# Work moved from the first expert pair to behind the seventh, and constants moved in the load order, in a hybrid attention and mixture-of-experts step

## The reference

```python
scores = sigmoid(t @ w_router)            # 64 experts, 8 picked for each token
a = silu(t @ w_exp_gate[e]) * (t @ w_exp_up[e]) * gate[e]
routed = sum_e a @ w_exp_down[e]          # 1024 -> 256 -> 1024 for each expert
shared = (silu(t @ w_sh_gate) * (t @ w_sh_up)) @ w_sh_down
return routed + shared
```

## Time and profile before

| | us |
|---|---|
| median of 3 runs | 787.26 (786.84 to 790.26) |
| profiled execution | 786.93 |
| its span | 785.1 |
| TensorE busy | 742.6 (95%) |
| VectorE busy | 383.4 (49%) |
| ScalarE busy | 136.3 (17%) |
| DMA | 268.72 MB, mean 342 GB/s |

### The profile page before, as it was taken

The page is one execution under the profiler, slowest core; times in us unless marked ns, Lnnn a source line. Parts: engine busy times, 40 slices in busy tenths (PEclk is TensorE's granted clock), DMA queues, the critical chain, the costliest instruction groups (busy, mean ns, idle before and its releaser), DMA issues.

```text
span 785.1 us, 13758 instructions
## 1 busy us (share of the span) xinstructions
PE 742.6 (95%) x5059; PEld 357.3 (46%) x5059; DVE 383.4 (49%) x869; ACT 136.3 (17%) x290; POOL 42.9 (5%) x49
## 2 busy tenths in 40 slices
PE   4999999889999999999999999899999999999988
PEld 0554434566555454544444444344444443444433
DVE  2236368483786334454454354344543454435456
ACT  3124001410111121111111111111110111111110
POOL 0000001000000110110100101101001011010100
PEclk9999999999999999999999999999999999999999
DMA  9993465650818969999999999999999999999992
GB/s 342 386 386 141 172 237 233 243 175 21 312 33 349 355 241 383 399 420 419 418 419 421 418 422 418 418 421 418 421 419 419 421 417 421 419 419 421 419 389 84
DMA packets 52218, 268.72 MB, mean 342 GB/s; under 512 B 6556, under 2 KB 8988, under 8 KB 27104
## 3 DMA queue, kind: packets, MB, share of 16 engines
q1 hardware_dynamic: 47584, 255.78, 81.0%
q0 software_dynamic: 4608, 12.59, 4.2%
HBM read 269.01 MB, written 3.52 MB: 347 GB/s over the span
## 4 chain that ended last, share of the span: by engine, by line
PE 59%; DMA 31%; DVE 5%; SPq 2%; issue 2%; ACT 1%; DVEq 0%; ACTq 0%
PE ps L555 55%; DMA raw_gu<-in_w_exp_up 29%; PE ps L1011 1%; DMA ada<-in_w_ada 1%; SPq L484 1%; SPq L485 0%; PE ps L866 0%; DVE probT L1624 0%; DVE x L1698 0%; PE ps L1038 0%; DVE xtmp L1696 0%; PE ps L632 0%; DVE h L1722 0%; DVE keyT L1569 0%; DVE h L1723 0%
## 5 line engine op out<-in xcount | busy, mean ns | idle before, releaser
L555 PE MATMUL ps<-raw_gu,xs 128*32 128x512 f32 x2048 | 226.1, 593 | 18.1 <-DMA raw_gu<-in_w_exp_up 16.7
L555 PEld LDWEIGHTS ps<-raw_gu,xs 128*32 128x32 f32 x2048 | 68.9, 110 | 172.5 <-issue 157.6
L555 PE MATMUL ps<-raw_dn,ast 128*32 128x512 f32 x824 | 116.3, 595 | 0.1
L1971 DVE TENSOR_TENSOR acc<-acc,ps 128x512 f32<-128x512 f32 x180 | 109.9, 678 | 0.0
L1928 DVE SCALAR_TENSOR_TENSOR act_a<-ps,small,sil 128x256 f32<-128x256 f32 x32 | 15.5, 484 | 192.1 <-ACT sil L1334 192.1
L555 PE MATMUL ps<-ys,place 128*128 128x512 f32 x360 | 98.4, 409 | 0.0
L555 PEld LDWEIGHTS ps<-ys,place 128*128 128x128 f32 x360 | 63.3, 189 | 35.7 <-issue 25.1
L1964 DVE TENSOR_TENSOR ys<-ps,ys 128x512 fp32r<-128x512 f32 x60 | 41.5, 691 | 66.0 <-ACT ys L1347 66.0
L555 PEld LDWEIGHTS ps<-raw_dn,ast 128*32 128x32 f32 x824 | 28.8, 109 | 60.4 <-issue 58.2
L1347 ACT CAST ys<-ps 128x512 fp32r<-128x512 f32 x60 | 35.1, 585 | 111.7 <-PE ps L555 111.7
L2080 POOL DMA_INDIRECT xg<-h_spill,slot_row x30 | 29.7, 988 | 435.5 <-DVE slot_row L1882 430.9
(11 more groups left out here) (319 smaller groups left out, 692.3 us busy)
## 6 DMA issues: line engine op xcount, KB each, us to landing
raw_gu<-in_w_exp_gate SPq DMA_DIRECT2D x64, 1024.0 KB, 16.0
raw_gu<-in_w_exp_up SPq DMA_DIRECT2D x64, 1024.0 KB, 18.1
raw_dn<-in_w_exp_down SPq DMA_DIRECT2D x48, 1024.0 KB, 16.8
ada<-in_w_ada SPq DMA_DIRECT2D x16, 512.0 KB, 11.3
ada2a<-in_w_ada SPq DMA_DIRECT2D x8, 1024.0 KB, 4.6
ada2b<-in_w_ada SPq DMA_DIRECT2D x8, 1024.0 KB, 6.2
raw_dn11a<-in_w_exp_down SPq DMA_DIRECT2D x16, 512.0 KB, 17.3
raw_dn11b<-in_w_exp_down SPq DMA_DIRECT2D x16, 512.0 KB, 21.1
```

What stands on the lines that cost most here:

```text
L555: return nc.tensor.matmul(out, l, r, start=first, stop=last)
L1971: V.tensor_tensor(a, a, ps[:, 4 + (6 * half + k) % 4, :], ALU.add).then_inc(S["acc_done"], 1)
```

## The change

`shared_down` and `over_tables` leave the first pair and come after the loop over pairs 1 to 6 (`SPLIT` = 7), in banks 4 to 7 (`rest`), with their own semaphores. VectorE takes them there: the tables as before, the shared sums as adds into `acc`; pair 0's first scattered sums are now copied into `acc` rather than added. The tables' readers wait there too, so each engine's main loop becomes two. `sh_aT` gets a place that stays free till then. Of `keep` only the unit matrix (64 KB) is loaded first, and the other 256 KB after `tconst`, behind the conditioning and first projection weights; the two waits for constants count to 80, not 64.

```diff
-        sh_aT = [at(f"sh_aT{t}", 74 + t, [P, 2, P]) for t in range(NT)]
+        sh_aT = [at(f"sh_aT{t}", (201, 202, 123)[t], [P, 2, P]) for t in range(NT)]
...
+        rest = ["overR", "overJ", "overK"] + [f"sd{t}{n}" for t in range(NT) for n in range(2)]
+        rest_no = {n: k for k, n in enumerate(rest)}
+        SPLIT = WIDE // 2 + 1
+
+        def rbank(n):
+            return ps[:, 4 + rest_no[n] % 4, :]
...
-            load(keep[:], A["c_keep"], "consts_in")
+            load(keep[:, 0:P], A["c_keep"][:, 0:P], "consts_in")
...
             load(tconst[:], A["c_trunk"], "consts_in")
+            load(keep[:, P:], A["c_keep"][:, P:], "consts_in")
...
-            sp.wait_ge(S["tables_ready"], 1)
-            n_pairs = sp.value_load(jobs[0:1, NJOB:NJOB + 1], min_val=NMAIN // 2, max_val=NUNIT // 2)
-            with sp.Fori(1, n_pairs - 1) as p:
...
+            with sp.Fori(1, SPLIT) as p:
+                next_weights(p)
...
+            def open_rest(n):
+                if rest_no[n] > 3:
+                    pe.wait_ge(S["rest_taken"], rest_no[n] - 3)
+                return rbank(n)
+
             def shared_down(t):
                 pe.wait_ge(S["shd_in"], 16)
-                pe.wait_ge(S["hr_sb"], hr_no[f"sa{t}"] + 1)
                 for n in range(2):
-                    o = open_hr(f"sd{t}{n}")
+                    o = open_rest(f"sd{t}{n}")
                     for f in range(2):
                         last = mm(o, sh_aT[t][:, f, :], w_shd[:, f, n * 512:(n + 1) * 512], f == 0, f == 1)
-                    last.then_inc(S["hr_done"], 1)
+                    last.then_inc(S["rest_done"], 1)
...
             shared_turn(2)
-            pe.wait_ge(S["hr_sb"], hr_no["sa2"] + 1)
-            shared_down(0)
             turn(0, 0, True)
-            over_tables()
-            shared_down(1)
             pe.wait_ge(S["misc_sb"], freed_all)
             pe.wait_ge(xg_in[1], 16)
             for n in range(2):
                 tokens_t(1, n)
-            shared_down(2)
             pe.wait_ge(S["pick_ready"], 2)
...
-            with pe.Fori(1, WIDE // 2 + 1) as p:
+            with pe.Fori(1, SPLIT) as p:
                 pair(p, True)
-            with pe.Fori(WIDE // 2 + 1, final) as p:
+            pe.wait_ge(S["xs_act"], 2 * SPLIT + 2)
+            pe.wait_ge(S["xs_dve"], 2 * SPLIT + 2)
+            over_tables()
+            for t in range(NT):
+                shared_down(t)
+            pe.wait_ge(S["tables_ready"], 1)
+            n_pairs = pe.value_load(jobs[0:1, NJOB:NJOB + 1], min_val=NMAIN // 2, max_val=NUNIT // 2)
+            final = pe.value_load(jobs[0:1, NJOB + 1:NJOB + 2], min_val=NMAIN // 2 - 1, max_val=NUNIT // 2 - 1)
+            pe.wait_ge(S["rest_taken"], len(rest))
+            with pe.Fori(SPLIT, final) as p:
...
-            def shared_out(t):
-                act.wait_ge(S["h2_out"], 16 * NT)
-                for n in range(2):
-                    act.wait_ge(S["hr_done"], hr_no[f"sd{t}{n}"] + 1)
-                    nc.scalar.copy(acc[:, t, n * 512:(n + 1) * 512], hbank(f"sd{t}{n}")).then_inc(S["hr_sb"], 1)
...
-            act.wait_ge(S["shared_done"], 1)
-            n_pairs = act.value_load(jobs[0:1, NJOB:NJOB + 1], min_val=NMAIN // 2, max_val=NUNIT // 2)
-            final = act.value_load(jobs[0:1, NJOB + 1:NJOB + 2], min_val=NMAIN // 2 - 1, max_val=NUNIT // 2 - 1)
...
+            with act.Fori(1, SPLIT) as p:
+                pair(p)
...
-            add_scattered(0, 1)
+            dve.wait_ge(S["h2_out"], 16 * NT)
+            for k in range(6):
+                dve.wait_ge(S["scat_done"], 6 + k + 1)
+                V.tensor_copy(acc[:, k // 2, k % 2 * 512:(k % 2 + 1) * 512], ps[:, 4 + (6 + k) % 4, :]).then_inc(S["acc_done"], 1)
...
+            def take_rest(n):
+                dve.wait_ge(S["rest_done"], rest_no[n] + 1)
+                return rbank(n)
+
+            def taken(i):
+                i.then_inc(S["rest_taken"], 1)
+
+            i = take_rest("overR")
+            own(V.tensor_copy(jobs[0:1, NE:NJOB], i[0:1, 0:NOVER]))
+            taken(V.tensor_scalar(pcmp[0:1], lc("four")[0:1], i[0:1, NOVER:NOVER + 1], None, ALU.is_lt))
+            dve.wait_ge(S["rest_taken"], 1)
+            own(V.tensor_reduce(pcount[0:1], pcmp[0:1], AX.X, ALU.add))
+            own(V.tensor_scalar(jobs[0:1, NJOB:NJOB + 1], pcount[0:1], float(NMAIN // 2), None, ALU.add))
+            own(V.tensor_scalar(jobs[0:1, NJOB + 1:NJOB + 2], pcount[0:1], float(NMAIN // 2 - 1), None, ALU.add))
+            i = take_rest("overJ")
+            V.memset(posq[:, :, QMAIN + QOVER:], -1.0)
+            taken(V.scalar_tensor_tensor(posq[:, :, QMAIN:QMAIN + QOVER], i[:, 0:NT * QOVER].rearrange("p (t j) -> p t j", t=NT), -1.0,
+                                         off[:, :, QMAIN:].to_broadcast([P, NT, QOVER]), ALU.add, ALU.subtract))
+            V.memset(gmov[:, :, NUNIT:, :].bitcast(F32), 0.0)
+            taken(gates(take_rest("overK"), NMAIN, NUNIT))
+            dve.wait_ge(S["rest_taken"], 3)
+            dve.sem_inc(S["tables_ready"], 1)
+            dve.wait_ge(S["acc_done"], 12 * SPLIT)
+            for t in range(NT):
+                for n in range(2):
+                    a = acc[:, t, n * 512:(n + 1) * 512]
+                    taken(V.tensor_tensor(a, a, take_rest(f"sd{t}{n}"), ALU.add))
+            n_pairs = dve.value_load(jobs[0:1, NJOB:NJOB + 1], min_val=NMAIN // 2, max_val=NUNIT // 2)
+            final = dve.value_load(jobs[0:1, NJOB + 1:NJOB + 2], min_val=NMAIN // 2 - 1, max_val=NUNIT // 2 - 1)
+            with dve.Fori(SPLIT, final) as p:
...
+            with pool.Fori(0, SPLIT) as p:
+                pool.wait_ge(S["xt_done"], 4 * p + 4)
+                gather(p + 1)
             pool.wait_ge(S["tables_ready"], 1)
             final = pool.value_load(jobs[0:1, NJOB + 1:NJOB + 2], min_val=NMAIN // 2 - 1, max_val=NUNIT // 2 - 1)
-            with pool.Fori(0, final) as p:
+            with pool.Fori(SPLIT, final) as p:
```

More of the change, by code:

```diff
@@ L346, in build @@
                  "score_ready mask_ready cnt_sb ownm_ready owner_ready jobs_ready tables_ready sh_sil_ready sh_a_ready "
-                 "begun weight_ready h21_taken x1_half sq_half xm_ready h2_out row_ready row_taken xt_done next_ready shared_done gt2_in scaled_sb high_sb low_sb z_ready y_ready y_out "
+                 "begun weight_ready h21_taken x1_half sq_half xm_ready h2_out row_ready row_taken xt_done next_ready rest_done rest_taken gt2_in scaled_sb high_sb low_sb z_ready y_ready y_out "
                  "first_pick first_gates first_row pick_ready gtmp_ready xs_act xs_dve gates_done slots_done place_ready up_done silu_done gated "
@@ L363, in build @@
                 + ["A20", "A21", "pv2", "mT10", "mT11", "o2", "mT20", "mT21"]
-                + ["pos", "key", "tabR", "tabP", "tabG", "tabJ", "tabK", "start", "overR", "overJ", "overK"])
+                + ["pos", "key", "tabR", "tabP", "tabG", "tabJ", "tabK", "start"])
         misc_no = {n: k for k, n in enumerate(misc)}
@@ L377, in build @@
         hr = [f"{n}{t}{x}" for t in range(NT) for n, x in (("h", 0), ("h", 1), ("r", ""))] \
-            + [f"sa{t}" for t in range(NT)] + [f"sd{t}{n}" for t in range(NT) for n in range(2)]
+            + [f"sa{t}" for t in range(NT)]
         hr_no = {n: k for k, n in enumerate(hr)}
@@ L544, in _ @@
                     load_dn(half, experts)
+            with sp.Fori(1, SPLIT) as p:
+                next_weights(p)
+            sp.wait_ge(S["tables_ready"], 1)
+            n_pairs = sp.value_load(jobs[0:1, NJOB:NJOB + 1], min_val=NMAIN // 2, max_val=NUNIT // 2)
+            with sp.Fori(SPLIT, n_pairs - 1) as p:
+                next_weights(p)
             for k, (n, t) in enumerate(last_order):
@@ L999, in over_tables @@
                     last = mm(w, ones[0:NE], offs[0:NE].unsqueeze(2).to_broadcast([NE, NOVER, 2]), False, True)
-                last.then_inc(S["misc_done"], 1)
-                o = open_misc("overK")
+                last.then_inc(S["rest_done"], 1)
+                o = open_rest("overK")
                 for t in range(NT):
@@ L1370, in _, with pair @@
             high_y(0, 1)
-            act.wait_ge(S["shared_done"], 1)
-            n_pairs = act.value_load(jobs[0:1, NJOB:NJOB + 1], min_val=NMAIN // 2, max_val=NUNIT // 2)
-            final = act.value_load(jobs[0:1, NJOB + 1:NJOB + 2], min_val=NMAIN // 2 - 1, max_val=NUNIT // 2 - 1)
-            with act.Fori(1, final) as p:
+            def pair(p):
                 silu(p, 0)
@@ L1384, in _ @@
                 high_y(p, 1)
+            with act.Fori(1, SPLIT) as p:
+                pair(p)
+            act.wait_ge(S["tables_ready"], 1)
+            n_pairs = act.value_load(jobs[0:1, NJOB:NJOB + 1], min_val=NMAIN // 2, max_val=NUNIT // 2)
+            final = act.value_load(jobs[0:1, NJOB + 1:NJOB + 2], min_val=NMAIN // 2 - 1, max_val=NUNIT // 2 - 1)
+            with act.Fori(SPLIT, final) as p:
+                pair(p)
```

(21 more changed lines are left out.)

21 lines of the change are left out of this document (6 added, 15 removed).

## The result

| | before | changed |
|---|---|---|
| median us (12 runs each) | 788.60 (786.84 to 791.57) | 783.12 (780.76 to 786.02) |
| ratio | | 0.9928 (95% interval 0.9914 to 0.9942) |
| profiled execution, its span | 786.93, 785.1 | 783.31, 781.5 |

The changed kernel is faster, by 5.5 us in the medians, where 8.3 were forecast; the interval of the ratio is clear of 1. The time goes with the mean granted clock: the changed kernel's four runs at 1.00 took 780.76 to 781.29 us, its eight at 0.996 to 0.998 took 782.81 to 786.02. The page of the changed kernel: the slice of 274 to 293 us, in which the weight stream stood still before, has 371 GB/s where it had 241, and a new dip has come, the 26th slice (488 to 508 us), with 302 GB/s where its neighbours have 420.

A forecast was written before the change was run, and what follows sets the result against it. The prediction took the weight stream as the bound behind 302 us, with TensorE close. Constants -0.6, stream gain -9.2 and new hole +1.5 sum to -8.3 from 787.26, taken as 778.8 us; range 776.2 to 783.0.

The forecast's parts named there:

- What bounds: Behind 302 us the weight stream is full, TensorE has little room; the one long stop, 284 to 296 us, is removable.
- TensorE in the first pair: Between the first two up products: 12.51 us of shared-down and table work removed, 0.16 exposed, net 12.35 us earlier.
- The stream's gain: Around 285 us: earlier requests for units 2 and 3 remove the stream's stop, worth 9.2 us (8.4 to 9.9).
- The block: After pair 6: tables and three shared_downs, 13.0 us; with last add and handovers the next up starts 14.0 us on.
- T0: The end of pair 6's last down product on TensorE, where the moved work starts; 490.79 us in the kernel before.
- rival C: At pair 7: engines entering new loops stall, widening the hole; slower than now, up to 791.5 us; chance 4%.
- a hole of 1.3 to 1.8; I take 1.5, ends 0 and 3: Weight stream after the moved work: idle between the queue's end and unit 16's data, costing 1.5 us.
- The queue lasts to T0 + 20.6 to 21.1.: Behind pair 6: after unit 14's weights land, 8.39 MB remain queued, keeping the stream busy 20.0 us.
- The start: Loading 256 KB of constants later brings the first conditioning pieces and the chain forward by 0.6 us (0.3 to 0.7).
- A: TensorE, not the stream, sets the end, so the work is moved but not hidden: 787.7 us, no change; chance 6%.
- B: At pair 7: late bank handover or engines running out unevenly opens a hole of 5 to 7 us: 783.5; chance 7%.
- D: The stop at 286 us merely shifts, another buffer being held; only 4 to 5 us return, 782.5 to 783; chance 8%.

The follow-up runs named there:

- e3_tables_only: The changed kernel without the three shared_downs and their adds, only the overflow tables left behind pair 6; 776.72 us, ratio 0.9845.
- e2_const_only: The kernel before with only the loading of the constants moved; 787.98 us, ratio 0.9977.
- after_again: The changed kernel run once more, unaltered, as the measure for the other runs on its chip; 781.71 us, ratio 0.9895.

## Why the prediction was right, and where it was off

**What bounds.** Right. The stop at 285 us was the only long one behind 284 us, its removal is what was won, and the end follows the last weights: the tail is 22.76 us in both. TensorE waits for weights again from unit 23, four and a half pairs behind the block, where the prediction had six without a wait. Of the slices, 21 and 33 GB/s are the lowest that the earlier trace rows shows, not 12 to 40, and 787.26 less 8.3 is 779.0; nothing hangs on either.

**TensorE in the first pair.** Forecast -12.35 at unit 1's up product; measured 26.38 to 13.44, -12.94. Of the 0.6 more, 0.5 lies in gate_slots(2), 0.74 from its start at 276.89 to the down product, where 1.24 was counted.

**The stream's gain.** Forecast 9.2 (8.4 to 9.9); measured 9.85 from unit 0 to unit 13, the end of the range that came from following each request to its landing, rather than from the idle share. First waits for weights came at unit 9, in pair 4, as forecast.

**The block.** The pause was forecast at 14.0 from T0 and measured at 14.2. VectorE's takes, timeline of VectorE (low_y, the last table and the last add):

```profile
482.95 0.69 DVE L1958 TENSOR_TENSOR ys<-ps,ys 128x512 fp32r<-128x512 f32 x1 [1.03 <-ACT ys L1358]
...
485.56 0.51 DVE L1881 TENSOR_TENSOR gmov<-ps,gmov 128x336 fp32r<-128x336 f32 x1
...
495.20 0.69 DVE L2056 TENSOR_TENSOR acc<-acc,ps 128x512 f32<-128x512 f32 x1 [1.03 <-PE ps L567]
```

The tables were done 3.9 us behind T0 (482.15), the last add 13.75. So rival C's stall by new code was not there in this kernel. The Trainium skill (Runtime: NRT & Kernel Launch, Instruction fetch mechanics) lets one expect a fetch where a branch leaves the prefetched pages; in the changed kernel's trace no such time can be seen, the pause is within 0.2 of the sum of its products and handovers. Whether the 2.1 us of e3_tables_only hold one is open.

**The step that failed** is the term "a hole of 1.3 to 1.8; I take 1.5, ends 0 and 3": the mechanism is as told, the size was 4.8 us of idle share, 5.2 in bytes. The cover was put at 12.5 us of pause (14.0 less 1.5); the runs give 9.6 by idle share. SyncE's request for unit 16's weights, timeline of SyncE:

```profile
503.60 0.34 SPq L490 DMA_DIRECT2D raw_gu<-in_w_exp_gate  x1
```

- The far end of the hole was right. The request came at T0 + 21.45, and by the share of 0.60 in the window from 504 data flowed at 504.8, T0 + 22.65, where T0 + 22.4 was forecast: 0.2 of the difference is the longer pause, and the restart, 1.4 us behind the up product's end, is that of before (1.33).
- "The queue lasts to T0 + 20.6 to 21.1." This is the part that failed. It counted 20.0 us of bytes, 8.39 MB, from the landing of unit 14's weights. But a landing is when the last engine is done; by then others had gone on to what is queued behind. From 482.75, T0 + 0.6, to 504 the mean is 338 GB/s, so only 7.2 MB were left: 1.2 MB, 2.9 us at 0.42 MB/us, had moved already. The last load before the hole lands late. From the view of the tile raw_dn11b, of its load issued at 483.31:

```profile
DMA to landing us min/median/max: 19.4/19.4/19.4
```

The load lands at 502.7, T0 + 20.6, just where the forecast put it. But the mean engine was out of work at 500.0, T0 + 17.9, 2.7 us before, as the windows above show (0.76, 0.24 and 0.01 busy). The Trainium skill (DMA: Bandwidth & Descriptors, Why a DMA increments its semaphore by 16 and not by 1) says that the engines of one transfer finish independently and that the semaphore counts them; the trace agrees, with an end spread over some 4 us. A landing is thus no point from which to count a queue's bytes; the windows of the DMA share are.

**The start.** Forecast 0.6; at the first conditioning pieces the lead was 1.27 in this pair of traces. Over all thirteen the fifth piece starts at 14.34 to 14.85 us with the move and at 15.54, 15.88 and 16.74 without it, so between the nearest two it is 0.69, which the bytes explain, and 1.4 in the mean, which they don't. What of it reaches the end stays open between 0.6 and 2 us.

**The rivals.** A (the pause shows in full) is refuted: 4.8 of 14.2 did. B (a hole of 5 to 7 because the engines run out unevenly) was nearest, at 7%: its second cause was the true one, and counted in bytes (5.2) so is its size. C and D didn't occur.

**The number.** 783.12 lies 0.1 us above the stated range (776.2 to 783.0). But the kernel before took 788.60 in these runs and not the 787.26 that the forecast starts from; the ratio carried over to 787.26 gives 781.6, inside, and at the very end of the sum's own range (776.7 to 781.6). That it lies well inside the stated one is owed to the width taken for rival D, which didn't occur, and in part to luck: the stream's gain, 0.65 us above its term, hides a fifth of the 3.3 us by which the hole was too small.

## What to carry to other kernels

Work taken out of a stretch where it holds up a stream is won nearly in full, and work put back where the stream is full is free only up to a length: what the queue holds, less the first product that frees a buffer and the restart (here 17.9 less 7.1 and 1.4, 9.4 us). Cut such work into pieces well below that (here pauses up to 7.3 us left no hole, one of 8.4 at a second stop left 0.7), and keep waits that nothing needs yet out of the pause. When reckoning how long a queue lasts, count bytes to the mean engine's end, not from or to a landing.

## What the runs showed of the hardware

- The 16 DMA engines empty a full queue over about 4 us: busy shares of 0.76, 0.24 and 0.01 in successive windows of 2 us, and the last landing 2.7 us behind the mean end.
- Behind an empty queue the stream came back the same way at 274 and at 504 us: the first packets 0.9 us after SyncE's first issue (273.59 and 503.60), by windows of 0.1 us, and the full rate 2.0 us after it.
- The granted clock fell to 0.50, the 1.2 GHz level, for some 3.5 us around 150 us in six of thirteen traces, the changed kernel's first among them; it cost 1.4 us there.
- In the first 20 us TensorE's products change from a wide to a close spacing at a moment that varies between executions: three transposes of 128 columns take 0.90 us before it and 0.55 behind it. That looks like a step from the lower to the upper level of the clock, but the records don't show it as one: the granted clock is 1.00 in every window of the first 30 us, which is the 2.4 GHz level. The last transposes of 0.90 us began at 16.84 in the kernel before, at 15.66 in e2_const_only and at 19.16 in the changed one, after 9 us without work and then short products with gaps of 0.3 us between them. Unit 0's up product began at 265.15 (after_again) and 267.65 us in two traces of one and the same kernel: 1.14 of the 2.50 us were there at the first projection (22.50 and 23.64), 1.36 came with the lower clock at 150 us.
- A whole load of 256 KB less in front brought the fifth conditioning piece forward by 1.27 us in the changed kernel's trace and by 1.18 in e2_const_only's, where its bytes at 386 GB/s are 0.68 us; but the three traces without the move differ among themselves by 1.20 us there.
